# Leading the U steps by 26 columns, the residual in DRAM, one-hots on GpSimd

## The chip, the core and the metric

One core of a Trainium2 chip runs the whole computation in one launch. The metric is the device time of one execution in microseconds. Before the change: median 2835.26 us of 3 runs (2834.31 to 2835.86).

## The reference

512 tokens of width 1024 go through two transformer blocks: the first with two kinds of attention and a gated feed-forward layer, the second with latent and forgetting attention and, in the place of its feed-forward layer, a mixture of single-vector experts. Only this last part is touched. All is float32.

```
qp = h @ w_pq                                  # 8 heads, 2 halves of 128
sc = einsum(qp, sub_keys)                      # 128 scores per head and half
s1, i1 = top_k(sc[0], 16); s2, i2 = top_k(sc[1], 16)
cand = s1[:, None] + s2[None, :]               # 256 sums, top 16 of them
expert = e1 * 128 + e2;  gate = softmax(top_s) # 8 x 16 = 128 slots per token
a = h . peer_u[expert];  w = gate * gelu(a)
y = sum over slots of w * peer_v[expert];  x = x + gate2 * y
```

## The kernel before

The tokens are four tiles of 128. Tiles 0 to 2 take the experts densely, tile 3 takes them sparsely, row by row.

**Dense part.** The 16384 experts are 128 columns of 128 (the column is the second key e2). For column j a *U step* loads `u_by_key[:, j, :]` (512 KB, ring `uraw` of UR = 3 slots), transposes it in two halves on TensorE (`u_transposes`), ScalarE rounds a half to `uT_hi` (`u_high`), VectorE makes the remainder `uT_lo` from PSUM (`u_low`), and TensorE multiplies by the tokens in three passes (`hidden`, 24 matmuls of 384 columns for both halves). `gelu` on ScalarE puts the result into `act_ring`, AHEAD slots of 384 columns. A *V half* (`experts_out`) takes column i's gates times its slot of the ring (`w_mul`), splits product and V column (`w_high`, `w_low`, `v_high`, `v_low`), and adds 18 matmuls of 512 columns into six PSUM banks. The main loop runs over i = 0 to 127 and does V half i and, while i + AHEAD is under 128, U step i + AHEAD. AHEAD is 16: the first 16 U steps run before the loop.

**Gates.** The dense gates are, per token, a 128 by 128 table with 128 entries that aren't zero. First VectorE finds the slots: for 8 heads and 3 tiles `key_tops` and `pair_tops` (one *round*), while TensorE still computes the scores of later heads. `tile_picks` looks the expert numbers up with one-hot tables `hot` of 128 x 2048 and normalises the gates; `slot_transposes` turns them, slot to partition. Then per tile NCH = 16 *chunks* of 8 tokens: VectorE makes `one1` (one instruction of 1024 columns, lines 1526) and eight `one2` (lines 1530, the gate times a one-hot), both in two buffers; TensorE multiplies them (16 matmuls, line 2050), ScalarE moves the result into `stage` (line 896). A tile's `stage` of 8 MB is stored to DRAM by `store_gates` in four transfers, and the next tile's first evacuation waits for them (`stage_free`). The loop reads the gates back, four columns at a time (`load_gates`).

**Where U steps stand before the loop.** One before the lookups, one after them, one after every fourth chunk, the last two after the last chunk.

**Queues.** All loads of U, V and gates and the stores of gates are issued by SyncE in one written order, each behind its own wait: U 0 to 8, store 0, U 9 to 11, store 1, U 12 to 15, store 2, V 0 to 2, gates 0 and 1, U 16 and 17, then the loop's loads. GpSimd has nothing to do between the projections and the loop; in the loop it issues the 256 indirect row loads of tile 3 (three buffers for U rows, three for V rows), whose dot products and sums VectorE makes at fixed steps 4 to 112 (`rows_at`). The last 24 rows in that order are all V rows. `finish3` closes tile 3 at step 112.

**The residual** x (4 x 1024 columns a partition) stays in SBUF throughout.

Of the kernel before, what the change touches and what calls it, by code (L numbers as in the profile page):

```python
# [15 lines left out]
P = 128  # L16
# [22 lines left out]
AHEAD = 16  # L39
# [34 lines left out]
def build(nc, wst, wada, x_in, meta_in, cols_in, rowsa_in, rowsb_in, rope_in, const_in, pos_in,  # L74
          subk_in, peer_u, peer_v, out):
    ctx = ExitStack()
    with ctx:
# [148 lines left out]
        keys = cut(r1, 10752, NKEYS)  # L226
# [7 lines left out]
        act_ring = cut(r2, 0, AHEAD, DN)  # L234
# [14 lines left out]
        hot = cut(big, 0, SLOTS, TOPK)  # L249
        ranks = cut(big, 2048, 2, SLOTS)  # L250
        rank_bits = cut(big, 2304, 2, SLOTS).bitcast(U32)
        topf = cut(big, 2560, 2, PH, TOPK)
        wrap = cut(big, 2816, SLOTS)
        picks = cut(big, 2944, DT, 2, SLOTS)
# [22 lines left out]
        u_by_key, v_by_key = (w.rearrange("(a b) d -> a b d", b=NKEYS) for w in (peer_u, peer_v))  # L277
        gd = nc.dram_tensor("gd", (DT, P, NKEYS * P), F32).ap()
# [55 lines left out]
        y_ready, y_out = sem("y_ready"), sem("y_out")  # L334
# [69 lines left out]

        block = ctx.enter_context(nc.Block())
# [3 lines left out]
        def _(sp):  # L409
# [46 lines left out]
            for j in range(12, 16):  # L456
# [7 lines left out]
            for j in range(AHEAD, AHEAD + 2):  # L464
                load_u(j)
            for i in range(NE):
                if i + AHEAD + 2 < NE:
                    load_u(i + AHEAD + 2)
# [5 lines left out]
            sp.dma_start(out[DT], x[:, DT, :]).then_inc(y_out, 16)  # L474
            for t in range(DT):
                sp.wait_ge(y_ready, t + 2)
                sp.dma_start(out[t], x[:, t, :]).then_inc(y_out, 16)
# [48 lines left out]


# [13 lines left out]
        def _(act):  # L541
# [313 lines left out]
            def gelu(j):  # L855
                act.wait_ge(a_acc, 2 * j + 2)
                if j >= AHEAD:
                    act.wait_ge(w_done, j - AHEAD + 1)
                act.activation(act_ring[:, j % AHEAD, :], ps[:, 0, 0:DN], ACT.Gelu_apprx_tanh,  # L859
                               bias=zero[:]).then_inc(a_ready, 1)  # L860
# [17 lines left out]
            for s in range(3):  # L878
                u_high(s)
            for t in range(DT):  # L880
                act.wait_ge(top_done, 8 * DT - DT + t + 1)
                act.activation(gate[:, t, :], gate[:, t, :], ACT.Exp, bias=zero[:]).then_inc(gate_exp, 1)
            gelu(0)
            for t in range(DT):
                slots_evac(t)
            u_high(3)
            u_high(4)
            gelu(1)
            for t in range(DT):
                stage_free(act, t)  # L890
                for c in range(NCH):
# [6 lines left out]
                    if c % 4 == 3:  # L898
                        j = 2 + 4 * t + c // 4
                        u_high(2 * j + 1)  # L900
                        u_high(2 * j + 2)
                        gelu(j)
            for j in range(2 + 4 * DT, AHEAD):
                u_high(2 * j + 1)
                u_high(2 * j + 2)
                if j < AHEAD - 1:
                    gelu(j)
# [32 lines left out]
        def _(v):  # L940
# [518 lines left out]

            def tile_picks(t):  # L1460

                v.tensor_copy(topf.rearrange("p a h k -> p (a h k)"), topi[:, t, :])
                pair_ranks(besti[:, t, :], rank_bits, ranks, wrap)
                for a in range(2):
                    v.tensor_tensor(hot, over(ranks[:, a, :], TOPK), each(iota, SLOTS), ALU.is_equal)
                    v.drain()
                    hk = hot.rearrange("p (h k) r -> p h k r", h=PH)
                    v.tensor_tensor(hk, hk, topf[:, a].unsqueeze(2).broadcast_to([P, PH, TOPK, TOPK]), ALU.mult)
                    v.drain()
                    v.tensor_reduce(picks[:, t, a, :], hot, AX.X, ALU.add)  # L1470
                    v.drain()
# [6 lines left out]
                v.tensor_tensor(g, g, over(gst[:, 1, PH * t:PH * t + PH], TOPK), ALU.mult)  # L1478
                v.drain().then_inc(picks_ready, 1)
# [11 lines left out]
            def w_mul(i):  # L1491
# [4 lines left out]
                if i >= 2:  # L1496
                    v.wait_ge(v_acc, i - 1)
                v.tensor_tensor(w_of[:, i % 2, :].rearrange("p (t n) -> p t n", t=DT), gring[:, b % 2, :, P * (i % GB):P * (i % GB) + P],
                                act_ring[:, i % AHEAD, :].rearrange("p (t n) -> p t n", t=DT), ALU.mult).then_inc(w_done, 1)
# [5 lines left out]

            for h in range(PH):
# [7 lines left out]
            for s in range(3):  # L1514
                u_low(s)
            for t in range(DT):
                tile_picks(t)
            u_low(3)
            u_low(4)
            for t in range(DT):  # L1520
                v.wait_ge(slot_ready, t + 1)
                for c in range(NCH):
# [5 lines left out]
                    for k in range(CHUNK):  # L1528
                        at = CHUNK * c + k
                        mk = v.tensor_scalar(one2[:, n % 2, k, :], keys, slotT[t][:, P + at:P + at + 1],  # L1530
                                             slotT[t][:, 2 * P + at:2 * P + at + 1], ALU.is_equal, ALU.mult)
                    mk.then_inc(one2_ready, 1)
                    if n and n % 4 == 0:
                        j = 1 + n // 4
                        u_low(2 * j + 1)
                        u_low(2 * j + 2)
            for j in range(1 + 4 * DT, AHEAD):
                u_low(2 * j + 1)
                u_low(2 * j + 2)
# [56 lines left out]
            def finish3():  # L1596
# [6 lines left out]
                v.tensor_tensor(x[:, DT, :], x[:, DT, :], yacc[:, 0, :], ALU.add).then_inc(y_ready, 1)  # L1603
# [5 lines left out]
            for i in range(NE):  # L1609
# [24 lines left out]
                if i == LAST_ROW:  # L1634
                    finish3()

            v.wait_ge(v_acc, NE)
            for t in range(DT):
# [3 lines left out]
                xt = x[:, t, :].rearrange("p (a b) -> p a b", a=2)  # L1642
# [4 lines left out]
        def _(pe):  # L1647
# [374 lines left out]
            def slot_transposes(t):  # L2022
# [4 lines left out]
                for k, src in enumerate((picks[:, t, 0, :], picks[:, t, 1, :], gate[:, t, :])):  # L2027
# [8 lines left out]
            experts_in(0)  # L2036
            for t in range(DT):
                slot_transposes(t)
            experts_in(1)
            for t in range(DT):  # L2040
                for c in range(NCH):
# [11 lines left out]
                    if c % 4 == 3:  # L2053
                        experts_in(2 + 4 * t + c // 4)
            for j in range(2 + 4 * DT, AHEAD):
                experts_in(j)
# [92 lines left out]
```

## Time and profile before

| what | us |
|---|---|
| median of 3 runs | 2835.26 |
| the profiled execution | 2836.87 |
| its span | 2834.8 |
| VectorE's first top-16 round | 1253.2 |
| first gate chunk on TensorE | 1452.3 |
| last gate chunk's end | 1670.5 |
| first instruction of the main loop | 1703.6 |

Busy shares of the span: TensorE 89%, VectorE 63%, ScalarE 34%, GpSimd 13%. The span is the time between the first and the last instruction that the profile shows. The shares are means over stages with different limits, so the rows further down are taken by stage.

In the rows, a window is given as start:end in us from the span's start, and then busy us and instructions in the order TensorE, its weight loads (PEld), VectorE (DVE), ScalarE (ACT), GpSimd (POOL). In a timeline, what stands in brackets is the idle time before the instruction and what ended it. SPq and POOLq are the queues in which SyncE and GpSimd issue transfers.

### The profile page before, as it was taken

Reading aid. Unit: us, or ns where it says so; the run is one execution under the profiler, and the core shown is the slowest. Engines: PE = TensorE matmul, PEld = TensorE weight load, DVE = VectorE, ACT = ScalarE, POOL = GpSimd, SP = SyncE. Lnnn points to the kernel's source line nnn. Section 1 sums busy time; section 2 is a strip of 40 time slices with the busy share of each in tenths; the row PEclk is TensorE's granted clock in tenths of the full one; section 3 lists DMA queues with packets and bytes.
Section 4 is the critical chain, followed back from the end, with each engine's and each line's share of the span. In section 5 each row is a group of like instructions: output and inputs, shape, how many; then the busy total and the mean of one; then the engine's idle time right before and its main releaser. Section 6 shows DMA issues by size and latency. Waiting matters only on the chain.

```text
span 2834.8 us, 37618 instructions
## 1 busy us (share of the span) xinstructions
PE 2533.6 (89%) x13697; PEld 2158.0 (76%) x13697; DVE 1786.0 (63%) x3871; ACT 956.0 (34%) x1637; POOL 354.6 (13%) x326
## 2 busy tenths in 40 slices
PE   8999888999989879989256669999999999999998
PEld 6777686777779757844156668898989898899986
DVE  5535646553254365458887657777777777777675
ACT  4334412222224445311134444333333333333332
POOL 1001100110000000100000001232222222222220
PEclk9999989999999989999678999999999999999999
DMA  4100014652222110030003345787777777778764
GB/s 174 73 31 1 1 62 170 227 203 90 89 74 75 60 45 1 1 126 1 8 23 141 149 175 186 266 291 262 269 261 269 268 265 267 268 272 276 247 222 141
DMA packets 107908, 427.20 MB, mean 151 GB/s; under 512 B 11328, under 2 KB 11584, under 8 KB 97104
## 3 DMA queue, kind: packets, MB, share of 16 engines
q1 hardware_dynamic: 62624, 262.17, 26.3%
q0 software_dynamic: 44064, 160.98, 16.2%
q8 instruction: 111, 1.82, 0.3%
q10 hardware_dynamic: 1040, 1.67, 0.2%
q14 instruction: 69, 0.57, 0.1%
HBM read 397.51 MB, written 27.26 MB: 150 GB/s over the span
## 4 chain that ended last, share of the span: by engine, by line
PE 74%; DVE 14%; issue 4%; ACT 3%; DMA 3%; DVEq 2%; ACTq 1%; SPq 1%; POOLq 0%
PE ps L2017 16%; PE ps L2001 16%; PE ps L1803 9%; PE ps L1757 7%; PE ps L1673 5%; PE ps L1825 4%; PE ps L1990 3%; PE ps L2050 3%; PE ps L1738 2%; DMA gd<-big 1%; PE ps L1942 1%; PE ps L1710 1%; PE ps L1924 1%; ACT r L638 1%; PE ps L1962 1%
## 5 line engine op out<-in xcount | busy, mean ns | idle before, releaser
L2001 PE MATMUL ps<-hd_hi,uT_hi 128*128 128x384 f32 x1024 | 349.9, 342 | 0.7 <-ACT r L859 0.7
L2001 PE MATMUL ps<-hd_hi,uT_lo 128*128 128x384 f32 x1024 | 348.1, 340 | 0.0
L2001 PE MATMUL ps<-hd_lo,uT_hi 128*128 128x384 f32 x1024 | 348.0, 340 | 0.0
L1483 DVE TENSOR_TENSOR uT_lo<-ps,uT_hi 128x512 fp32r<-128x512 f32 x256 | 176.7, 690 | 256.0 <-ACT uT_hi L840 255.8
L2017 PE MATMUL ps<-v_hi,ew_hi 128*128 128x512 f32 x768 | 320.5, 417 | 2.6 <-DVE v_lo L1488 2.1
L2017 PE MATMUL ps<-v_hi,ew_lo 128*128 128x512 f32 x768 | 303.1, 395 | 0.0
L2017 PE MATMUL ps<-v_lo,ew_hi 128*128 128x512 f32 x768 | 300.9, 392 | 0.0
L840 ACT ACTIVATE uT_hi<-ps 128x512 fp32r<-128x512 f32 x256 | 153.1, 598 | 268.8 <-PE ps L1990 268.8
L536 POOL DMA_INDIRECT big<-peer_u,r x128 | 135.3, 1057 | 861.8 <-DVE r L1558 523.5
L859 ACT ACTIVATE r<-ps,zero 128x384 f32<-128x384 f32 x128 | 74.4, 581 | 472.4 <-PE ps L2001 468.1
L1990 PE MATMUL ps<-const,r 128*128 128x128 f32 x1024 | 155.7, 275 | 52.6 <-DVE uT_lo L1483 33.5
L2001 PEld LDWEIGHTS ps<-hd_hi,uT_hi 128*128 128x128 f32 x1024 | 194.0, 189 | 10.0 <-issue 1.1
L2001 PEld LDWEIGHTS ps<-hd_hi,uT_lo 128*128 128x128 f32 x1024 | 193.7, 189 | 9.6
L2001 PEld LDWEIGHTS ps<-hd_lo,uT_hi 128*128 128x128 f32 x1024 | 193.7, 189 | 0.0
L536 POOL DMA_INDIRECT big<-peer_v,r x128 | 144.3, 1127 | 386.2 <-DVE big L1586 369.9
L1488 DVE TENSOR_TENSOR v_lo<-r,v_hi 128x1024 fp32r<-128x1024 f32 x128 | 156.8, 1225 | 34.1 <-ACT v_hi L847 34.1
L1990 PEld LDWEIGHTS ps<-const,r 128*128 128x128 f32 x1024 | 126.7, 141 | 65.7 <-DVE uT_lo L1483 25.5
L1586 DVE SCALAR_TENSOR_TENSOR big<-big,r 128x1024 f32<-128x1024 f32 x128 | 164.5, 1285 | 15.4 <-DMA big<-peer_v,r 3.1
L2017 PEld LDWEIGHTS ps<-v_hi,ew_lo 128*128 128x128 f32 x768 | 144.2, 188 | 32.7
L2017 PEld LDWEIGHTS ps<-v_hi,ew_hi 128*128 128x128 f32 x768 | 144.7, 188 | 26.8 <-DVE v_lo L1488 3.4
L2017 PEld LDWEIGHTS ps<-v_lo,ew_hi 128*128 128x128 f32 x768 | 145.2, 189 | 24.3
L1068 DVE TENSOR_TENSOR w_lo<-big,w_hi 128x2048 fp32r<-128x2048 f32 x42 | 96.2, 2290 | 106.2 <-ACT w_hi L631 106.2
(330 smaller groups left out, 5325.2 us busy)
## 6 DMA issues: line engine op xcount, KB each, us to landing
big<-wst SPq DMA_DIRECT2D x70, 1024.0 KB, 4.9
r<-peer_u SPq DMA_DIRECT2D x128, 512.0 KB, 7.4
r<-peer_v SPq DMA_DIRECT2D x128, 512.0 KB, 5.3
r<-wada POOLq DMA_DIRECT2D x48, 512.0 KB, 4.6
gd<-big SPq DMA_DIRECT2D x12, 2048.0 KB, 14.1
big<-gd SPq DMA_DIRECT2D x32, 768.0 KB, 9.2
x<-x_in SPq DMA_DIRECT2D x4, 512.0 KB, 6.8
big<-peer_u,r POOLq DMA_INDIRECT x128, 6.6
```

The source lines that it names most:

```text
L536: pool.indirect_dma_start(rows[n % RW], None, table, bass.IndirectOffsetOnAxis(ap=idx[:, n:n + 1], axis=0)).then_inc(got[n % RW], 16)
L840: act.activation(uT_hi[:, s % 2], ps[:, 1, :].rearrange("p (k n) -> p k n", k=KD // 2), ACT.Copy).then_inc(u_hi_done, 1)
L1483: v.tensor_tensor(uT_lo[:, s % 2], ps[:, 1, :].rearrange("p (k n) -> p k n", k=KD // 2), uT_hi[:, s % 2].bitcast(F32), ALU.subtract).then_ ...
L1488: v.tensor_tensor(v_lo[:, i % VR, :], vraw[:, i % VR, :], v_hi[:, i % 2, :].bitcast(F32), ALU.subtract).then_inc(v_lo_done, 1)
L1586: v.scalar_tensor_tensor(out=yacc[:, n % 2, :], in0=vrows[n % RW], scalar=wts[:, n:n + 1], in1=yacc[:, n % 2, :], op0=ALU.mult, op1=ALU.ad ...
L1673: mm = pe.matmul(ps[0:r, bank, 0:w], hT[:, k, t * P:t * P + r], wt[:, k, 0:w], start=(k == 0), stop=(k == KD - 1))
L1757: mm = pe.matmul(ps[:, bank, 0:256], h[:, k, t * P:(t + 1) * P], w[:, k, :], start=(k == 0 and i == 0), stop=(k == KD - 1 and i == 2))
L1803: mm = pe.matmul(ps[:, 2 * (f % 2) + u, :], w[:, k, u, :], h[:, k, 0:512], start=(k == 0 and i == 0), stop=(k == KD - 1 and i == 2))
L1825: mm = pe.matmul(ps[:, 2 * t + half, :], a[:, f % 2, t * P:(t + 1) * P], w[:, f % 2, 512 * half:512 * half + 512], start=(f == 0 and i == ...
L1990: mm = pe.transpose(ps[:, 1, P * k:P * k + P], uraw[:, j % UR, at:at + P], ident)
L2001: mm = pe.matmul(ps[:, 0, 0:DN], w[:, k, :], h[:, KD // 2 * half + k, :], start=(half == 0 and k == 0 and i == 0), stop=(half == 1 and k = ...
L2017: mm = pe.matmul(ps[:, 2 + 2 * t + half, :], w[:, P * t:P * t + P], vv[:, 512 * half:512 * half + 512], start=(i == 0 and n == 0), stop=(i ...
```

## The change

- AHEAD is 26. The ring's first ten slots lie in the buffer of the residual x; x is stored to DRAM (`xd`) when the attention's output has been added, and read back (`xback`) at step 116, when tile 3's row buffers are free. ScalarE waits for the store before its first `u_high`.
- U steps before the loop: 11 ahead of the first gate chunk (`u_low` 0 stands before head 6's rounds, then two U steps' `u_low`s behind each of five of the last six rounds, one more behind `tile_ranks(0)`), four in a block behind tile 0's chunks, four behind tile 1's, seven behind tile 2's. None between chunks.
- `tile_picks` is cut in two. `tile_ranks` makes the ranks and, for tile 0, both one-hot tables; `tile_picks` normalises the gates, multiplies and reduces both tables in one instruction. One of tile 0's multiplies runs on GpSimd. The lookups of tiles 1 and 2 stand in VectorE's queue behind `one1` of tile 0's chunks 3 and 8.
- The eight `one2` of every chunk are made by GpSimd; `one1` stays on VectorE.
- SyncE's order: U 0 to 2, the stores of x, U 3 to 13, gates 0, U 14 to 17, gates 1, U 18 to 21, gates 2, V 0 to 2, U 22 to 26, gate loads 0 and 1, U 27 and 28, then the loop's.
- `finish3` is at step 122, after a wait for x.

```diff
-AHEAD = 16
+AHEAD = 26
+INX = 10
+BEFORE = (11, 15, 19, 26)
-        act_ring = cut(r2, 0, AHEAD, DN)
+        x_flat = x.rearrange("p t d -> p (t d)")
+        act_ring = ([x_flat[:, DN * s:DN * s + DN] for s in range(INX)]
+                    + [r2[:, DN * (AHEAD - 1 - s):DN * (AHEAD - s)] for s in range(INX, AHEAD)])
...
# SyncE
-            for j in range(9):
+            for j in range(UR):
+                load_u(j)
+            sp.wait_ge(out_add, 8 * T)
+            for t in range(T):
+                sp.dma_start(xd[t], x[:, t, :]).then_inc(x_out, 16)
+            for j in range(UR, BEFORE[0] + UR):
                 load_u(j)
             store_gates(0)
-            for j in range(9, 12):
+            for j in range(BEFORE[0] + UR, BEFORE[1] + UR):
                 load_u(j)
             store_gates(1)
...
             for i in range(VR):
                 load_v(i)
+            for j in range(BEFORE[2] + UR, AHEAD + 1):
+                load_u(j)
             for b in range(2):
                 load_gates(b)
...
+                if i == LAST_ROW + 4:
+                    sp.wait_ge(u_row, SLOTS)
+                    sp.wait_ge(v_row, SLOTS)
+                    sp.wait_ge(x_out, 16 * T)
+                    for t in range(T):
+                        sp.dma_start(xback[t], xd[t]).then_inc(x_back, 16)
# GpSimd
+            pool.wait_ge(ranks_ready, 1)
+            hk = hot[:, 0].rearrange("p (h k) r -> p h k r", h=PH)
+            pool.tensor_tensor(hk, hk, each_pick(0), ALU.mult).then_inc(hot_ready, 1)
+            for t in range(DT):
+                pool.wait_ge(slot_ready, t + 1)
+                for c in range(NCH):
+                    n = t * NCH + c
+                    if n >= 2:
+                        pool.wait_ge(g_acc, 2 * (n - 1))
+                    for k in range(CHUNK):
+                        at = CHUNK * c + k
+                        mk = pool.tensor_scalar(one2[:, n % 2, k, :], keys, slotT[t][:, P + at:P + at + 1],
+                                                slotT[t][:, 2 * P + at:2 * P + at + 1], ALU.is_equal, ALU.mult)
+                    mk.then_inc(one2_ready, 1)
# ScalarE
+            def hidden_evac(j):
+                u_high(2 * j + 1)
+                u_high(2 * j + 2)
+                gelu(j)
...
+            act.wait_ge(x_out, 16 * T)
+            u_high(0)
+            for j in range(8):
+                hidden_evac(j)
+            gate_exps(0)
+            for j in range(8, 10):
+                hidden_evac(j)
+            gate_exps(1)
+            gate_exps(2)
+            hidden_evac(10)
+            slots_evac(0)
...
# VectorE
+            def tile_ranks(t):
+                v.tensor_copy(topf.rearrange("p a s -> p (a s)"), topi[:, t, :])
+                pair_ranks(besti[:, t, :], rank_bits, ranks, wrap)
+                if t == 0:
+                    for a in range(2):
+                        rank_hot(a).then_inc(ranks_ready, 1)
...
             for h in range(PH):
                 v.wait_ge(sk_ev, 2 * h + 2)
+                if h == PH - 2:
+                    u_low(0)
                 for t in range(DT):
                     key_tops(t, h)
                     v.drain()
                     pair_tops(t, h).then_inc(top_done, 1)
+                    if h >= PH - 2:
+                        u = DT * (h - PH + 2) + t
+                        hidden_low(range(2 * u, min(2 * u + 2, 10)))
+            tile_ranks(0)
+            hidden_low([10])
...
+                    if t == 0 and c in (3, 8):
+                        tile_ranks(c // 5 + 1)
+                        tile_picks(c // 5 + 1)
+                    if t and c == 1:
+                        hidden_low(range(BEFORE[t - 1], BEFORE[t]))
+            hidden_low(range(BEFORE[DT - 1], AHEAD))
# TensorE
+            for j in range(BEFORE[0]):
+                experts_in(j)
+            slot_transposes(0)
...
-                    if c % 4 == 3:
-                        experts_in(2 + 4 * t + c // 4)
+                    if t == 0 and c in (9, 13):
+                        slot_transposes((c - 5) // 4)
+                for j in range(BEFORE[t], BEFORE[t + 1]):
+                    experts_in(j)
```

## Rows read from the trace of the kernel before

**Rows 1.** Windows: length, busy us per engine, granted clock, DMA share, GB/s.

```profile
1253.20:1382.60 129.40, 103.66 (x325) 51.73 (x323) 114.18 (x643) 16.72 (x28) 0.00 (x0) 0.92 0.06 21
1382.60:1450.00 67.40, 16.54 (x73) 15.04 (x73) 53.74 (x63) 8.28 (x14) 0.00 (x0) 0.58 0.05 16
1452.26:1512.13 59.87, 48.59 (x354) 45.99 (x355) 53.92 (x147) 35.15 (x40) 0.00 (x0) 0.97 0.09 27
1512.13:1591.90 79.77, 53.99 (x386) 51.45 (x385) 56.58 (x154) 37.46 (x45) 0.00 (x0) 0.89 0.34 132
1670.54:1703.56 33.02, 13.30 (x81) 12.28 (x79) 3.46 (x5) 4.90 (x9) 0.00 (x0) 0.78 0.95 376
1703.56:2745.00 1041.44, 1032.71 (x5559) 936.37 (x5560) 780.42 (x1311) 365.47 (x590) 279.59 (x256) 1.00 0.75 261
2753.00:2819.40 66.40, 64.28 (x281) 52.31 (x281) 38.63 (x49) 22.59 (x31) 0.00 (x0) 1.00 0.49 155
```

**Rows 2.** The chain that ended last: start us, us, what.

```profile
1450.06 2.05 DVE r L1530 x8
...
1515.62 20.73 DMA gd<-big
...
1594.89 20.20 DMA gd<-big
...
1682.76 20.76 DMA r<-peer_u
```

**Rows 3.** VectorE timeline: start us, us, engine, line, operation, tiles, shapes.

```profile
1392.68 2.29 DVE L1465 TENSOR_TENSOR big<-big,const 128x2048 f32<-128x2048 f32 x1
...
1448.85 1.22 DVE L1526 TENSOR_TENSOR r<-r,gates 128x1024 f32<-128x1024 f32 x1
...
1452.03 1.22 DVE L1526 TENSOR_TENSOR r<-r,gates 128x1024 f32<-128x1024 f32 x1
1453.16 2.13 DVE L1530 TENSOR_SCALAR r<-r,gates 128x128 f32<-128x128 f32 x8
```

**Rows 4.** ScalarE timeline: first uT_hi, then two gelus back to back.

```profile
1359.45 0.60 ACT L840 ACTIVATE uT_hi<-ps 128x512 fp32r<-128x512 f32 x1 [1.03 <-PE ps L1990]
...
1675.75 0.58 ACT L859 ACTIVATE r<-ps,zero 128x384 f32<-128x384 f32 x1 [1.51 <-PE ps L2001]
...
1681.42 0.58 ACT L859 ACTIVATE r<-ps,zero 128x384 f32<-128x384 f32 x1 [1.51 <-PE ps L2001]
```

**Rows 5.** TensorE's timeline: a gate chunk, and the loop's first transposes.

```profile
1461.77 2.02 PE L2050 MATMUL ps<-r 128*128 128x128 f32 x16 [1.16 <-issue]
...
1703.56 1.12 PE L1990 MATMUL ps<-const,r 128*128 128x128 f32 x4 [19.07 <-DMA r<-peer_u]
```

**Rows 6.** GpSimd timeline; last a group of lines (busy us, mean ns).

```profile
329.57 1.89 POOL L489 CAST w_hi<-big 128x2048 fp32r<-128x2048 f32 x1 [57.43 <-ACTq L641]
331.55 4.52 POOL L491 TENSOR_TENSOR w_lo<-big,w_hi 128x2048 fp32r<-128x2048 f32 x1
336.01 2.37 POOL L489 CAST w_hi<-big 128x2048 fp32r<-128x2048 f32 x1
...
L515 POOL MEMSET r<- 128x8 f32 x1 | 0.1, 116 | 4.1 <-issue 4.1
```

**Rows 7.** VectorE's timeline, line 1096: alone, and beside GpSimd's subtract.

```profile
300.37 0.77 DVE L1096 SCALAR_TENSOR_TENSOR r<-r,coef 128x528 f32<-128x528 f32 x1
...
334.02 2.61 DVE L1096 SCALAR_TENSOR_TENSOR r<-r,coef 128x528 f32<-128x528 f32 x1
```

**Rows 8.** Page groups (busy us, mean ns); last, DMA issues of 2700:2750.

```profile
L536 POOL DMA_INDIRECT big<-peer_v,r x128 | 144.3, 1127 | 386.2 <-DVE big L1586 369.9
L1488 DVE TENSOR_TENSOR v_lo<-r,v_hi 128x1024 fp32r<-128x1024 f32 x128 | 156.8, 1225 | 34.1 <-ACT v_hi L847 34.1
...
L1586 DVE SCALAR_TENSOR_TENSOR big<-big,r 128x1024 f32<-128x1024 f32 x128 | 164.5, 1285 | 15.4 <-DMA big<-peer_v,r 3.1
...
big<-peer_v,r POOLq DMA_INDIRECT x12, 5.6
```

More of the change, by code:

```diff
@@ L248, in build @@
         slotT = [gates[:, 0, 0:384], gates[:, 0, 384:768], r1[:, 10240:10624]]
[L249 to L254, printed above, removed]
+        xback = [cut(big, 8192 + D * i, D) for i in range(T)]
+        hot = cut(r2, 0, 2, SLOTS, TOPK)
+        rank_bits = cut(r2, 14368, 2, SLOTS).bitcast(U32)
+        ranks = cut(r2, 14624, 2, SLOTS)
+        wrap = cut(big, NKEYS * P, SLOTS)
+        topf = cut(r1, 11104, 2, SLOTS)
+        picks = [v.rearrange("p (a s) -> p a s", a=2) for v in (gates[:, 0, 768:1024], r1[:, 10848:11104], rowsb[:, 0:256])]
         gring = cut(big, 0, 2, DT, GB * P)
@@ L1458, in pair_ranks, with rank_hot @@
                 v.drain()
-            def tile_picks(t):
[L1462 to L1471, printed above, removed]
+            def rank_hot(a):
+                v.tensor_tensor(hot[:, a], over(ranks[:, a, :], TOPK), each(iota, SLOTS), ALU.is_equal)
+                return v.drain()
+            def tile_ranks(t):
[4 more added lines that the diff above has]
+                        rank_hot(a).then_inc(ranks_ready, 1)
+            def tile_picks(t):
                 v.wait_ge(gate_exp, t + 1)
@@ L1478, in tile_picks @@
                 v.tensor_tensor(g, g, over(gst[:, 1, PH * t:PH * t + PH], TOPK), ALU.mult)
+                for a in ((0, 1) if t else (1,)):
+                    if t:
+                        rank_hot(a)
+                    hk = hot[:, a].rearrange("p (h k) r -> p h k r", h=PH)
+                    v.tensor_tensor(hk, hk, each_pick(a), ALU.mult)
+                    v.drain()
+                if t == 0:
+                    v.wait_ge(hot_ready, 1)
+                v.tensor_reduce(picks[t], hot, AX.X, ALU.add)
                 v.drain().then_inc(picks_ready, 1)
@@ L1504, in w_low, with hidden_low @@
                                 ALU.subtract).then_inc(ew_lo_done, 1)
+            def hidden_low(steps):
+                for j in steps:
+                    u_low(2 * j + 1)
+                    u_low(2 * j + 2)
             for h in range(PH):
                 v.wait_ge(sk_ev, 2 * h + 2)
+                if h == PH - 2:
+                    u_low(0)
                 for t in range(DT):
@@ L1511, in _ @@
                     pair_tops(t, h).then_inc(top_done, 1)
+                    if h >= PH - 2:
[3 more added lines that the diff above has]
+            hidden_low([10])
             v.wait_ge(keys_acc, 1)
             v.tensor_scalar(keys, ps[:, 2, 0:NKEYS], 1.0, None, ALU.subtract)
[L1514 to L1519, printed above, removed]
+            v.drain()
+            tile_picks(0)
             for t in range(DT):
@@ L2026, in slot_transposes @@
                     pe.wait_ge(slot_ready, t - 1)
-                for k, src in enumerate((picks[:, t, 0, :], picks[:, t, 1, :], gate[:, t, :])):
+                for k, src in enumerate((picks[t][:, 0, :], picks[t][:, 1, :], gate[:, t, :])):
                     mm = pe.transpose(ps[:, 2 + t % 2, P * k:P * k + P], src, ident)
@@ L2052, in _ @@
                         mm.then_inc(g_acc, 1)
[L2053 to L2056 removed]
+                    if t == 0 and c in (9, 13):
+                        slot_transposes((c - 5) // 4)
+                for j in range(BEFORE[t], BEFORE[t + 1]):
+                    experts_in(j)
             for i in range(NE):
```

68 lines of the change are left out of this document (23 added, 45 removed).

## The prediction

> **What bounds the kernel now.** I read the busy time by stage first. In the loop over key columns TensorE is the bound: 112 steps in about 1041 us, 9.3 us each, and after them 16 steps without a U half in 66.4 us, 4.15 us each [rows 1]. Before that loop it is not: 1253 to 1450 us is VectorE's stretch, and in the gate stage TensorE is busy for 48.6 of 59.9 us of tile 0 and 54.0 of 79.8 of tile 1. The chain of waits names what ends last there [rows 2]: VectorE's one-hot builds, two 20 us waits while 8 MB of gates are stored, and a 20.8 us transfer of a U column queued behind the third store, for which TensorE idles 19.1 us [rows 5]. VectorE gives its prices [rows 1, 3]: one top-16 round 5.39 us (24 rounds in 129.4), one pass over a 2048-wide one-hot 2.29 us, and per chunk of 8 experts one1 1.22 us and eight one2 2.13 us, pitch 3.18 us. TensorE's 16 matmuls of a chunk are 2.02 us [rows 5], so the chunk is VectorE's. One U step back to back takes 5.67 us, gelu to gelu [rows 4].
>
> I sum against the profiled execution (2836.87 us, span 2834.8), which is 1.6 us above the median 2835.26.
>
> **Term 1, up to the first gate chunk.** VectorE starts u_low(0) ahead of head 6, about 18 rounds after 1253.2, at 1350.2. But ScalarE makes the first uT_hi at 1359.45 [rows 4], behind all score evacuations, and that order is kept. VectorE waits and is done at 1360.8, 10.6 us lost. Then six rounds (32.3 us) with five groups of four u_lows. The first of a group finds its input ready (0.69 us); the three others wait for transposes, the 2.1 us of matmuls, gelu and ScalarE: about 7.5 us. Five groups are 41 us. Between groups TensorE pauses some 2.5 us; a transpose batch after a pause took 1.12 us, and the clock was 0.58 over the pauses of 1382 to 1450 [rows 1, 5]; I add 7 us. That is 1441. tile_ranks(0) with two hots 6.8; the eleventh step's two u_lows 3; gate sums, one multiply (2.29) and one 4096-wide reduction (two passes, 4.5) 8.5; slot transposes and evacuation 1.5: 1460. GpSimd's one multiply there costs 4.5 us [rows 6], hidden by those u_lows but for a fraction. GpSimd then needs a first chunk of one2, and TensorE starts it at 1463 instead of 1452.3: +10.7 us, with 11 U steps done instead of 2.
>
> **Term 2, the pitch of a chunk.** The trace has no tensor_scalar on GpSimd. Its ends: a one-input pass costs 1.89 us for 2048 elements and a tiny one 0.116, so 128 elements are 0.23 us; by the two-input pass (4.52) 0.39 [rows 6]. It has one tensor input but two operations and two per-partition scalars, so I take 0.30, between the ends. Now the shared access: VectorE's two-input L1096 takes 0.77 us alone and 2.61 when it starts during GpSimd's subtract; it ends 0.56 after that one, and GpSimd's next cast takes 2.37 instead of 1.89 [rows 6, 7]. So the two take turns. one1 has two SBUF inputs and runs once per chunk, 1.15 us taken from GpSimd. Pitch: 8 x 0.30 + 1.15 = 3.55 us, ends 2.96 and 4.27, against 3.18 now. Moving one2 gains nothing, since the free VectorE can't hurry GpSimd.
>
> The Trainium skill says the same of the pair ("SBUF — State Buffer", Who interferes with whom): an exclusive lock, held for a whole instruction, also against a VectorE instruction with two SBUF inputs. By its figure for one-input work ("GPSIMD Engine Reference", Engine selection: roughly line rate) the pitch would be at my lower end.
>
> **Term 3, the gate stage.** Tile 0: 15 pitches + 2.0 = 55.3. The lookups of tiles 1 and 2 stand in VectorE's queue ahead of the next one1: 17 us each (four passes 9.4, reduction 4.5, the rest 3) and 1 for turns. GpSimd can only be two chunks ahead, since one2 has two buffers. Chunk 4 starts 19.2 us after chunk 3's one1, chunk 6's one2 begins 2.2 later: a delay of 21.4 - 2 x 3.55 = 14.3 us, twice 28.6. Tile 0 ends at 1463 + 83.9 = 1546.9.
>
> Between tiles four U steps run in a block. The ring has three U columns; the fourth is issued behind the 8 MB store. Two steps take 12 us, the third stops at 14.9 in the transposes of column 14. The store is issued 1.2 after the last chunk and lands some 23 us later (20.7 in flight, rows 2), the column at 25.7: 10.8 us idle. Then 2.6 + 5.7 + 2 (low clock) = 36 us to the next tile's first chunk. The tile: 36 + two prepared chunks 4.1 + 14 x 3.55 = 89.8 us; now tile 1 takes 79.8 [rows 1] and tile 2 the same (its store's wait starts 79.3 us after the first's, rows 2), also with four U steps each, because there the steps lie mostly inside VectorE's pitch. Ends: 1636.7 and 1726.5.
>
> After tile 2, seven U steps. Two run, the third waits for a column that is issued behind the store and three V columns, which lands at about 28 us; then 2.6 + 2 + 4 x 5.67 = 27.3. The loop begins at 1726.5 + 55.3 = 1781.8 instead of 1703.56: **+78.2 us**.
>
> **Term 4, the loop.** Ten U steps fewer: steps 102 to 111 have only the V half, 4.15 us of TensorE instead of 9.26. But tile 3's rows go on to step 112, 256 rows over 108 steps = 2.37 a step, and the last 24 are all V rows through three buffers: issue 1.13, landing 5.6 from issue, VectorE 1.29 [rows 8], with hand-overs about 8 us for three, 6.4 us a step. (VectorE's own sum is below: 2.37 x 1.29, v_low 1.23 and two 384-wide passes near 0.5 each, 5.3.) So the saving is 10 x (9.26 - 6.4) = **-28.6**, ends -20 and -38. The residual's 2 MB read at step 116 puts a V load about 5 us later, which had about as much slack: +1. Its store at 1260 us is beside projections: 0. finish3's three passes move into equal steps: 0.
>
> Sum: 78.2 - 28.6 + 1 = +51; 2836.87 + 51 - 1.6 = **2886 us** (on the median's footing).
>
> Each 0.1 us of one2 is 0.8 us a chunk; in the terms above about 40 pitches count, 32 us. Ends: 0.23 gives 2862, 0.39 gives 2915. The ends of term 1 (0 to +16 for clock and pauses) and of term 4 add about 15 to each side.
>
> **Rivals.**
> A, faster: GpSimd keeps ahead and TensorE is the chunk's bound, at 2.1 us. It decides where eight one2 and their turns are below 2.3 us, so 0.23 each and no turns with one1. 40 x (3.55 - 2.1) = 58 less: 2828. For it: TensorE needs only 2.02; against it: rows 7. Chance 0.14.
> B, GpSimd is much dearer: the per-partition scalars are fetched anew for each instruction, one2 at 0.5 us, pitch 5.15, 40 x 1.6 = 64 more: 2950. For it: no row shows such an instruction, and the small ones have a fixed share of 0.1; against: nothing here shows a fixed share that large. Chance 0.16. The Trainium skill ("GPSIMD Engine Reference", Performance pitfalls for Q7 kernels) charges each small read about 102 cycles; by that two scalars would add 0.17 us to 0.23, near 0.40, between the forecast and B.
> C, the column isn't held by the store (it overtakes): 2 x 10.8 + 11 less, 2854. Against: TensorE's 19.1 us wait [rows 5]. Chance 0.08.
> D, the change doesn't put lookups beside gates in a useful way: this is already in the sum (28.6 us). If they hid wholly: 2858, chance inside the forecast's low side.
>
> The forecast with its ends: chance 0.62, 2862 to 2915. Faster by over 0.2% (what this kernel's measurement can tell, 5.7 us) holds most of A and little of C: 0.15; within 0.2%: 0.04; slower 0.81. Range 2828 to 2945: below lies half of A, above most of B's half.
>
> **What would show it.** Right: eight one2 on GpSimd fill the chunk, with one1 lengthened; u_low(0) waits about 10 us; a stop of TensorE near 11 us on a peer_u transfer within each block between tiles; two 14 us holes in tile 0; steps 102 to 111 above 6 us. First gate chunk near 1463, loop near 1782. Wrong: a chunk pitch under 3 us, or a loop start before 1725 (then it is faster), or steps 102 to 111 at 4.2 us (22 us better).

## The result, and the profile after

The change makes the kernel slower: 3046.2 us median of 4 runs (3045.8 to 3051.3) against 2835.6 (2834.3 to 2836.1, one run more than ahead of the prediction), ratio 1.075; the brackets give the 95% interval, [1.074, 1.077]. The forecast was 2886 us, with a range from 2828 to 2945. The sign was right and most places were right; one price was wrong by a factor of 2.6, and it was paid for 48 chunks.

The windows of the changed kernel by stage (length, then busy us of TensorE, weight loads, VectorE, ScalarE, GpSimd, granted clock, DMA share, GB/s), to lay beside [rows 1]:

```profile
1253.20:1382.60 129.40, 122.66 (x412) 67.97 (x411) 96.61 (x530) 23.13 (x38) 0.00 (x0) 0.97 0.13 45
1382.60:1474.87 92.27, 52.64 (x287) 48.07 (x285) 54.54 (x159) 21.45 (x34) 12.96 (x10) 0.81 0.16 52
1474.87:1599.20 124.33, 59.66 (x263) 55.84 (x264) 51.89 (x45) 33.24 (x33) 124.33 (x125) 0.60 0.00 0
1599.20:1634.40 35.20, 23.07 (x130) 21.91 (x129) 6.76 (x9) 7.11 (x12) 9.66 (x12) 0.84 0.74 298
1634.40:1741.70 107.30, 54.57 (x259) 51.37 (x258) 18.48 (x15) 32.60 (x32) 105.27 (x118) 0.64 0.00 0
1741.70:1777.20 35.50, 24.08 (x130) 22.93 (x130) 6.76 (x9) 7.11 (x12) 9.60 (x12) 0.83 0.74 296
1777.20:1883.00 105.80, 54.05 (x258) 50.75 (x257) 17.36 (x14) 32.56 (x32) 100.53 (x112) 0.66 0.00 0
```

The three long windows are the tiles' chunks. In tile 0 GpSimd is busy for 124.33 of 124.33 us, TensorE for 59.66, VectorE for 51.89. Where VectorE bounded the chunks before, GpSimd does now, without a gap. The group on the page and GpSimd's timeline over tile 0 (start, duration, what) say it again (the first row of the timeline is the one multiply, 4.48 us for 4.5 forecast). The page's mean of 971 ns holds the turns with VectorE as well, in which the two engines wait for each other:

```profile
L563 POOL TENSOR_SCALAR r<-r,gates 128x128 f32<-128x128 f32 x256 | 243.9, 971 | 42.7 <-PE ps L2110 27.6
```

```profile
1446.83 4.48 POOL L554 TENSOR_TENSOR r<-r 128x2048 f32<-128x2048 f32 x1 [225.92 <-DVEq L1509]
1466.39 94.00 POOL L563 TENSOR_SCALAR r<-r,gates 128x128 f32<-128x128 f32 x89 [15.08 <-ACT gates L915]
```

TensorE's timeline of the changed kernel, to lay beside [rows 5]. Lines 2110 are a chunk's 16 matmuls, 2051 the transposes of a U step:

```profile
1474.87 3.75 PE L2110 MATMUL ps<-r 128*128 128x128 f32 x16 [9.11 <-POOL r L563]
1482.11 3.75 PE L2110 MATMUL ps<-r 128*128 128x128 f32 x16 [3.49 <-POOL r L563]
1489.39 3.75 PE L2110 MATMUL ps<-r 128*128 128x128 f32 x16 [3.52 <-issue]
1502.81 3.75 PE L2110 MATMUL ps<-r 128*128 128x128 f32 x16 [9.67 <-issue]
...
1545.04 3.75 PE L2110 MATMUL ps<-r 128*128 128x128 f32 x16 [9.45 <-issue]
...
1624.85 0.69 PE L2051 MATMUL ps<-const,r 128*128 128x128 f32 x2 [11.15 <-DMA r<-peer_u]
...
1912.86 0.69 PE L2051 MATMUL ps<-const,r 128*128 128x128 f32 x2 [15.56 <-DMA r<-peer_u]
```

From 1474.87 to 1482.11 is 7.24 us: the pitch of a chunk, 3.18 before. The two longer gaps (9.67 and 9.45) are the lookups of tiles 1 and 2, then come the stops on a U column behind a store. Only the first two gaps name GpSimd; the others are put down to "issue". The chain of waits alone would mislead here, since it follows TensorE, VectorE's one1 and then "issue":

```profile
1482.11 3.77 PE ps L2110 x16
1485.90 1.27 DVE r L1592
1487.17 2.21 issue
1489.39 3.75 PE ps L2110 x16
1493.14 9.67 issue
```

one1 waits for the buffer that the chunk before frees, and the "issue" behind it is the time in which GpSimd finishes its eight. The windows' GpSimd column is what settles it.

The gap of 9.67 us is made by the two engines' turns. While VectorE makes and multiplies the one-hot tables of a lookup (four passes with two inputs), GpSimd gets one instruction done per pass (GpSimd's row, then VectorE's of the same time):

```profile
1489.27 11.11 POOL L563 TENSOR_SCALAR r<-r,gates 128x128 f32<-128x128 f32 x5
```

```profile
1490.14 2.28 DVE L1508 TENSOR_TENSOR r<-r,const 128x2048 f32<-128x2048 f32 x1
...
1497.33 2.38 DVE L1532 TENSOR_TENSOR r<-r 128x2048 f32<-128x2048 f32 x1
```

Five one2 take 11.11 us, where five alone take 3.9. The same happens to VectorE ahead of the gates: its two one-hot tables of tile 0 take 9.05 us, where one alone is 2.29 [rows 3], because GpSimd's multiply (4.48 us from 1446.83) starts ahead of the second.

```profile
1444.41 9.05 DVE L1508 TENSOR_TENSOR r<-r,const 128x2048 f32<-128x2048 f32 x2
```

The first `uT_lo` of VectorE with its wait, and the waits from 2894.16 to 2966.76, ten steps without a U half (engine, line, what it waited for: us in total, times, longest):

```profile
1364.57 0.69 DVE L1541 TENSOR_TENSOR uT_lo<-ps,uT_hi 128x512 fp32r<-128x512 f32 x1 [8.97 <-ACT uT_hi L879]
```

```profile
POOL big L575 <- DVE big L1646: 43.4, 15, 7.3
PEld ps L2078 <- DVE v_lo L1546: 22.9, 9, 6.2
PE ps L2078 <- DVE v_lo L1546: 18.8, 7, 5.8
...
DVE big L1646 <- DMA big<-peer_v,r: 6.9, 4, 2.9
```

There TensorE waits for VectorE, whose queue holds the row work between the V halves. Ten such steps take 72.6 us; the same ten, still with their U halves, took 90.9 before:

```profile
2662.40:2753.33 90.93, 90.93 (x491) 82.51 (x490) 64.52 (x76) 29.73 (x49) 24.37 (x22) 1.00 0.71 248
```

### The profile page after: what moved, and what is told of

Its sections match the earlier page's. It is cut to its first block, busy times and chain, and to the rows that moved or that the text cites. A ratio compares the mean times of both kernels' runs of the same rounds, so it can differ in the third digit from the quotient of the medians.

```text
span 3049.5 us, 37605 instructions
## 1 busy us (share of the span) xinstructions
PE 2629.1 (86%) x13697; PEld 2237.1 (73%) x13697; DVE 1696.9 (56%) x3483; ACT 967.5 (32%) x1640; POOL 722.6 (24%) x711
## 4 chain that ended last, share of the span: by engine, by line
PE 73%; DVE 11%; issue 6%; ACT 3%; DMA 3%; DVEq 1%; POOL 1%; ACTq 1%; SPq 0%
PE ps L2062 14%; PE ps L2078 14%; PE ps L1864 8%; PE ps L1818 6%; PE ps L2110 5%; PE ps L1734 5%; PE ps L1886 4%; PE ps L2023 4%; PE ps L2051 3%; DMA r<-peer_u 2%; DVE r L1592 2%; PE ps L1799 2%; PE ps L1771 1%; PE ps L2003 1%; PE ps L1985 1%
## 5 line engine op out<-in xcount | busy, mean ns | idle before, releaser
L2110 PE MATMUL ps<-r 128*128 128x128 f32 x768 | 167.6, 408 | 178.3 <-issue 165.7
L2110 PEld LDWEIGHTS ps<-r 128*128 128x128 f32 x768 | 156.8, 312 | 189.0 <-issue 189.0
L563 POOL TENSOR_SCALAR r<-r,gates 128x128 f32<-128x128 f32 x256 | 243.9, 971 | 42.7 <-PE ps L2110 27.6
L944 ACT ACTIVATE big<-ps 128x512 f32<-128x512 f32 x96 | 99.8, 1053 | 247.6 <-PE ps L2110 247.6
```

The lines of the kernel that those rows point to most:

```text
L563: mk = pool.tensor_scalar(one2[:, n % 2, k, :], keys, slotT[t][:, P + at:P + at + 1], slotT[t][:, 2 * P + at:2 * P + at + 1], ALU.is_equal ...
L2110: mm = pe.matmul(ps[:, 4 + u % 4, P * k:P * k + P], one1[:, n % 2, 4 * half + k, :], one2[:, n % 2, 4 * half + k, :], start=True, stop=True)
```

## The experiments

**One2 back on VectorE, the rest of the change kept.** The eight `tensor_scalar` move from GpSimd's list to behind `one1`:

```diff
-                        mk = pool.tensor_scalar(one2[:, n % 2, k, :], keys, ...
+                        mk = v.tensor_scalar(one2[:, n % 2, k, :], keys, ...
```

> The changed kernel with only the eight one2 of a chunk back on VectorE. Theory S (a GpSimd one2 at 0.905 us was the mis-sized term, the rest of the sum stands): chunk pitch near 3.2 us instead of 7.24, two lookups in tile 0 that cost about 14 us each, two blocks of 35 us between tiles, loop steps 102 to 111 at 7.3 us; 2875 to 2895 us, still slower than before. Rival R (the one2 hid a good change: the ten U steps moved out of the loop pay): below 2830 us.

Measured: 2888.7 us (2885.3 to 2889.7), ratio 1.018 [1.016, 1.020]; theory S holds and rival R falls. So GpSimd's share of the loss is 157.5 us of 210.6, and the rest of the change costs 53. TensorE's timeline of this kernel (its gate line is 2104):

```profile
1470.12 2.02 PE L2104 MATMUL ps<-r 128*128 128x128 f32 x16 [1.60 <-issue]
1473.30 2.02 PE L2104 MATMUL ps<-r 128*128 128x128 f32 x16 [1.16 <-issue]
1493.49 5.44 PE L2104 MATMUL ps<-r 128*128 128x128 f32 x32 [18.17 <-issue]
...
1526.76 3.76 PE L2104 MATMUL ps<-r 128*128 128x128 f32 x16 [17.82 <-issue]
...
1574.35 0.47 PE L2045 MATMUL ps<-const,r 128*128 128x128 f32 x1 [8.01 <-DMA r<-peer_u]
```

The pitch is 3.18 again. Here the lookups are dear, gaps of 18.2 and 17.8 us for 1.2 to 1.6 elsewhere, so about 17 us each, the forecast's own price of a lookup: with one2 behind them in the same queue nothing is prepared meanwhile. "Lookups beside the gate matmuls" hides almost nothing of them. The last row is the stop behind tile 0's store, there without GpSimd too.

**The kernel before, with one2 on GpSimd alone.** The same move in the other direction:

```diff
+                        mk = pool.tensor_scalar(one2[:, n % 2, k, :], keys, ...
-                        mk = v.tensor_scalar(one2[:, n % 2, k, :], keys, ...
```

> The kernel before with only the eight one2 of a chunk on GpSimd, nothing else of the change. Theory S: chunk pitch near 7.2 us, three tiles near 120 to 130 us each with U steps hidden under GpSimd's time, so the gate stage 150 to 160 us longer: 2980 to 3000 us. Rival R (the pitch comes from the change's order of lookups and U steps around the chunks): under 2900 us.

Measured: 2960.9 us (2958.7 to 2964.7), ratio 1.044 [1.042, 1.045], far above rival R's 2900 and 19 us below the expectation's low end. The pitch of this kernel, on TensorE's timeline:

```profile
1488.35 3.75 PE L2057 MATMUL ps<-r 128*128 128x128 f32 x16 [4.34 <-issue]
1495.58 3.75 PE L2057 MATMUL ps<-r 128*128 128x128 f32 x16 [3.48 <-issue]
```

It is 7.23 us, as in the changed kernel, so the price comes with the eight one2 on GpSimd (and one1 beside them) and from nothing else in the change. Nearly the whole cost follows: 48 chunks at 7.24 are 348 us, where the three tiles took 59.9 + 79.8 + about 79.3 = 219 with their U steps [rows 1, 2]. That is +129; +125.3 was measured. The U steps between the chunks cost nothing now, because TensorE does them while GpSimd works. The expectation had that, but took 120 to 130 us for a tile where 16 pitches are 116.

**What makes the instruction dear: three kernels with other forms.** Each takes the changed kernel, gives GpSimd another form in each tile, and leaves `one1` out from chunk 2 on (8 columns are written in its place), so that outside the lookups hardly anything takes turns with GpSimd. What they compute is no longer the gates; only their traces are read.

```diff
-                    v.tensor_tensor(one1[:, n % 2], each(keys, CHUNK), ...
+                    if n < 2: (as before)
+                    else: v.tensor_scalar(one1[:, n % 2, 0, 0:8], keys[:, 0:8], 0.0, None, ALU.add)
# first kernel: tile 0 as in the change; tile 1 constants; tile 2 twice as wide, 4 a chunk
+                            mk = pool.tensor_scalar(one2[:, n % 2, k, :], keys, 5.0, 0.5, ALU.is_equal, ALU.mult)
+                            mk = pool.tensor_scalar(one2[:, n % 2, 2 * k:2 * k + 2, :], each(keys, 2), ...
# second kernel: tile 0 one comparison; tile 1 with a constant; tile 2 two inputs
+                            mk = pool.tensor_scalar(..., keys, slotT[t][:, P + at:P + at + 1], None, ALU.is_equal)
+                            mk = pool.tensor_scalar(..., keys, 5.0, None, ALU.is_equal)
+                            mk = pool.tensor_tensor(..., keys, slotT[t][:, ...].broadcast_to([P, NKEYS]), ALU.mult)
# third kernel: tile 0 a multiply; tile 1 twice as wide; tile 2 a wide comparison
+                            mk = pool.tensor_scalar(one2[:, n % 2, k, :], keys, 0.5, None, ALU.mult)
```

> The changed kernel, one1 left out from chunk 2 on (an 8-column one-input write stands for it). Tile 0: one2 as it is. Tile 1: both scalars are constants in the instruction. Tile 2: per-partition scalars, four instructions of 256 columns for eight of 128. Theory F (fetching two per-partition scalars is a fixed cost): tile 0 at 0.90 us each, tile 1 at 0.25 to 0.45, tile 2 at 1.0 to 1.1. Rival E (two operations on each element are slow): tile 1 stays at 0.9, tile 2 near 1.7. Rival T (turns with VectorE's one1): tile 0 falls to 0.76 and the pitch from 7.24 to 6.1 us.

> As the run before, one1 left out. Tile 0: one comparison with one per-partition scalar. Tile 1: one comparison with a constant. Tile 2: a two-input multiply of 128 columns. Theory F: tile 0 midway between 0.9 and the constants' time (0.55 to 0.7 us), tile 1 0.25 to 0.4, tile 2 near 0.39. Rival E: tile 0 and tile 1 alike, near 0.5.

> GpSimd's forms again, one1 left out, gates meaningless. Tile 0: one multiply by a constant, 128 columns; tile 1: the same, 256 columns; tile 2: one comparison with a constant, 256 columns. Two-input multiplies of 128 columns took 0.36 us, comparisons 0.59. Theory C (the comparison is the slow part): tile 0 near 0.25 us, tile 1 near 0.36, tile 2 near 0.95. Theory G (every tensor_scalar takes this slow path, whatever its operation): tile 0 near 0.59, tile 1 and 2 alike, 0.9 to 1.0.

Measured: 2973.4, 2917.5 and 2890.1 us, one run each. What counts is GpSimd's timeline, one stretch of back-to-back instructions after another; a stretch divided by its count is one instruction. First kernel:

```profile
1615.90 78.90 POOL L567 TENSOR_SCALAR r<-r 128x128 f32<-128x128 f32 x112 [30.39 <-PE ps L2119]
...
1736.07 67.23 POOL L569 TENSOR_SCALAR r<-r 128x256 f32<-128x256 f32 x56 [31.55 <-PE ps L2119]
```

Second kernel:

```profile
1591.45 66.24 POOL L566 TENSOR_SCALAR r<-r 128x128 f32<-128x128 f32 x112 [30.60 <-PE ps L2118]
...
1697.87 14.33 POOL L568 TENSOR_TENSOR r<-r 128x128 f32<-128x128 f32 x40 [34.34 <-PE ps L2118]
```

Third kernel:

```profile
1518.20 26.23 POOL L563 TENSOR_SCALAR r<-r 128x128 f32<-128x128 f32 x53
...
1584.41 45.63 POOL L565 TENSOR_SCALAR r<-r 128x256 f32<-128x256 f32 x56 [33.45 <-PE ps L2116]
...
1669.90 51.07 POOL L567 TENSOR_SCALAR r<-r 128x256 f32<-128x256 f32 x56 [32.53 <-PE ps L2116]
```

A stretch of tile 0 counts only outside the two lookups, whose passes stretch GpSimd's instructions; the third kernel's row starts behind the second lookup. For the first two kernels I take TensorE's pitch of a chunk over 8: 6.18 us in the first, 4.63 in the second (3.95 in the third, the same 0.49 as its row). In us per instruction:

| GpSimd instruction | 128 columns | 256 columns |
|---|---|---|
| two operations, two per-partition scalars (the change) | 0.773 | 1.20 |
| two operations, two constants | 0.705 | |
| one comparison, per-partition scalar | 0.578 | |
| one comparison, constant | 0.592 | 0.912 |
| one multiply, constant | 0.494 | 0.815 |
| multiply of two inputs, the second one column repeated | 0.358 | |

Four things follow. Leaving one1 out shortens the chunk by 7.24 - 6.18 = 1.06 us, so the two do take turns, at the forecast's 1.15 but for a tenth (rival T of the first expectation). The scalars in memory aren't the price: 0.773 against 0.705 with both constant, and 0.578 against 0.592, so theory F falls. A doubled width adds 0.32 to 0.43, so 128 columns carry a part that no width explains, if cost grows in a straight line between the two widths: 0.773 - (1.20 - 0.773) = 0.35 us of the change's instruction, 0.27 of the comparison, 0.17 of the lone multiply. And the operation counts: a comparison costs 0.10 more than a multiply at either width, and the second operation some 0.11, so the third expectation's theory G (every form alike, near 0.59) is wrong as well as its theory C (0.25). Every one-input form is dearer than the two-input one, the reverse of [rows 6]. Why that is so stays open, and no run made one2 of wide two-input passes.

The second kernel's tile 0 shows a lookup again: its second one delays the next chunk to 12.07 us after the last, at a pitch of 4.63.

```profile
1506.99 2.02 PE L2118 MATMUL ps<-r 128*128 128x128 f32 x16 [1.27 <-DVE r L1601]
1519.06 1.20 PE L2118 MATMUL ps<-r 128*128 128x128 f32 x4 [10.05 <-issue]
```

**Tile 3's rows earlier.** The kernel with one2 on VectorE, and one more edit:

```diff
-FIRST_ROW, LAST_ROW = 4, 112
+FIRST_ROW, LAST_ROW = 4, 101
```

> The run with one2 on VectorE, and the last of tile 3's 256 rows at step 101 instead of 112 (2.6 rows a step; finish3 and the read of x move along by 11 steps). Theory S (steps 102 to 111 are held by V rows through three buffers, 7.3 us each where TensorE needs 4.15): those steps fall to 4.2 us and the whole by 25 to 32 us, to about 2860 us. Rival L (the rows cost the same wherever they stand, because the loop's VectorE or DMA has no room): no gain, 2880 to 2890 us.

Measured: 2875.4 us (2871.2 to 2878.0), ratio 1.014 [1.012, 1.017]; 13.3 less than without it, half of what theory S expected. Windows of the first (112) and the second (101): steps 2 to 50, then ten steps without a U half.

```profile
1786.83:2233.98 447.15, 443.28 (x2392) 401.55 (x2391) 340.93 (x622) 161.56 (x259) 120.96 (x112) 1.00 0.77 264
2728.71:2804.40 75.69, 52.44 (x196) 40.23 (x195) 52.53 (x57) 15.18 (x21) 26.96 (x22) 0.86 0.72 245
```

```profile
1789.01:2250.28 461.27, 448.75 (x2401) 405.12 (x2400) 363.76 (x683) 165.06 (x262) 137.95 (x124) 0.99 0.78 270
2745.44:2793.49 48.05, 47.03 (x207) 38.20 (x206) 26.93 (x34) 15.33 (x21) 0.00 (x0) 1.00 0.58 198
```

The ten late steps fall from 75.7 to 48.1 us, all that was hoped for (27.6). But the 48 early ones rise by 14.1: 12 more row DMAs and 23 us more of VectorE stand in them (some of tile 3's top-16 searches come along with the rows), and TensorE, busy for 443.3 of 447.2 before, now has 12.5 us without work, all of it waiting for `uT_lo`. The rate of 2.6 rows a step alone doesn't explain it: the next 50 steps take up 11 more row DMAs and rise by only 2.8 us (466.6 to 469.4).

**U columns between the parts of a store.** On the kernel with one2 on VectorE (behind tile 2, gate load 0 also moves ahead of V 1 and 2):

```diff
-            store_gates(0)
-            for j in range(BEFORE[0] + UR, BEFORE[1] + UR):
-                load_u(j)
+                store_quarter(t, 0)
+                store_quarter(t, 1)
+                load_u(a + UR)
+                store_quarter(t, 2)
+                load_u(a + UR + 1)
+                store_quarter(t, 3)
...
```

> The run with one2 on VectorE, and the U columns a block needs issued between the four quarters of a tile's gate store instead of behind it; after tile 2 the first gate columns ahead of V 1 and 2. Theory S (a block stops 8 to 12 us, the last one 15 us, for a column behind the store): the stops on peer_u go, blocks take 25 us instead of 36, and the time falls by 25 to 35 us, to about 2858 us. Rival W (the stores only move the stop: the next tile's first evacuation then waits as long): under 8 us of gain.

Measured: 2862.1 us (2858.9 to 2869.2), ratio 1.009 [1.006, 1.011]: 26.6 less by the medians, 19.6 by the profiled spans (2867.4 and 2887.0). TensorE's waits for a U column between the gate stage and the loop, without the edit and with it:

```profile
PE ps L2045 <- DMA r<-peer_u: 32.2, 3, 15.4
```

```profile
PE ps L2052 <- DMA r<-peer_u: 10.9, 3, 8.4
```

21.3 us of stops are gone, and the loop begins 19.0 earlier, nearly all of the 19.6 of the spans; the rest of the 26.6 lies within the spread of the runs. Rival W falls. Between the tiles the columns were held by the order of SyncE's queue: the stops of 8.0 and 8.8 us are gone. Behind tile 2 some 10 us are left of 15.4.

**All of it put in another order.** Lead 26 is kept. one2 and all lookups are VectorE's and the lookups stand ahead of the first chunk, with `u_low`s put singly between their pieces; 14 U steps are ahead of the gate stage; `u_low(0)` is behind round 20 of 24 and not ahead of round 19, so that it needn't wait so long; the stores are split; rows end at 101.

```diff
-BEFORE = (11, 15, 19, 26)
-FIRST_ROW, LAST_ROW = 4, 112
+BEFORE = (14, 18, 22, 26)
+FIRST_ROW, LAST_ROW = 4, 101
-                    if t == 0 and c in (3, 8):
-                        tile_ranks(c // 5 + 1)
-                        tile_picks(c // 5 + 1)
+            for t in range(DT):
+                tile_ranks(t)
+                next_low()
+                tile_picks(t)
...
```

> The lead of 26 kept, everything around it reordered: one2 and all lookups on VectorE ahead of the gates, single u_lows between the pieces of the rounds and lookups so that VectorE does not wait (14 U steps ahead of the gates), u_low 0 only behind round 20, blocks of four U steps with split stores, rows done at step 101. Theory S by its own terms: first gate chunk near 1475 us, chunk pitch 3.2, blocks of 25, loop start near 1710, 102 x 9.3 + 26 x 4.15 behind it: 2775 to 2795 us, faster than before by 40 to 60. Rival: each u_low between pieces waits for TensorE's 2.8 us pace and the first gate chunk comes 15 us later, 2800 us.

Measured: 2787.8 us (2785.8 to 2790.3), ratio 0.983 [0.981, 0.985]. It is 1.7% faster than the kernel before and beats the changed one by 8.5%. Its windows: up to the first chunk, tile 0, and the block behind it.

```profile
1382.60:1458.78 76.18, 63.50 (x357) 55.84 (x357) 68.50 (x103) 24.10 (x41) 0.00 (x0) 0.98 0.24 76
1458.78:1508.80 50.02, 33.27 (x255) 31.02 (x256) 49.49 (x139) 29.48 (x31) 0.00 (x0) 0.97 0.00 1
1508.80:1533.70 24.90, 21.48 (x132) 20.36 (x131) 10.06 (x23) 7.55 (x13) 0.00 (x0) 1.00 0.92 369
```

The first chunk starts 16 us before the changed kernel's, with three U steps more behind it; tile 0 takes 50.0 instead of 124.3, the block 24.9 instead of 35.2. The loop's first multiply is at 1688.26; before it was at 1705.95. The expectation's 2775 to 2795 was met partly by luck: the loop starts some 20 us earlier than its 1710, and the loop's steps are slower than its 9.3 us (steps 2 to 50 take 9.57).

**The same with rows to step 112,** to see whether the early rows pay there too:

```diff
-FIRST_ROW, LAST_ROW = 4, 101
+FIRST_ROW, LAST_ROW = 4, 112
```

> The reordered kernel (lead 26, one-hots and lookups on VectorE ahead of the gates, 14 U steps ahead of the first gate chunk, U columns between the parts of a store) with tile 3's rows spread to step 112 again instead of 101. By the two runs that differ in this alone under the other order (2888.7 with 112, 2875.4 with 101), theory E (early rows pay in the tail what they cost in part in the loop, independent of the order ahead of the loop): steps 2 to 50 at 9.31 us instead of 9.57, steps 101 to 111 at 7.3 to 8.3 instead of 5.35, together 2796 to 2806, so 10 to 15 slower than 2787.8. Theory F (the slower loop steps of the reordered kernel come from something else than the rows, so that they stay near 9.57): 2808 to 2820.

Measured: 2802.8 us (2800.1 to 2803.5), ratio 0.988 [0.986, 0.990]; 15.0 more. Steps 2 to 50 and ten late steps:

```profile
1700.05:2147.56 447.51, 443.55 (x2394) 401.83 (x2393) 341.22 (x622) 161.60 (x259) 121.92 (x112) 1.00 0.78 264
2642.14:2715.82 73.68, 53.72 (x198) 40.67 (x197) 52.56 (x58) 15.18 (x21) 30.22 (x22) 0.88 0.75 255
```

The ten late steps take 73.7 us instead of 48.0, steps 2 to 50 take 447.5 instead of 459.5. So the exchange is the same in both orders: 26 to 28 us won late for 12 to 14 given early. The slower early steps come from the rows and what moves with them (theory E).

## Why the prediction was wrong, point by point

The stages from the first chunk to the loop, in us:

| | forecast | measured |
|---|---|---|
| start of the first gate chunk | 1463 | 1474.9 |
| tile 0's chunks | 83.9 | 124.3 |
| block of four U steps | 36 | 35.2 |
| tile 1's chunks | 53.8 | 107.3 |
| block of four U steps | 36 | 35.5 |
| tile 2's chunks | 53.8 | 105.8 |
| from there to the loop | 55.3 | 54.2 |
| the loop starts later by | 78.2 | 233.7 |

**The step that failed: Term 2, "so I take 0.30, between the ends".** One `tensor_scalar` of 128 columns costs GpSimd 0.773 us alone and 0.905 with the turns; the pitch is 7.24, not 3.55, and not within the ends either (4.27). The forecast's own rule, 40 pitches, gives 40 x 3.69 = 148 us more, 2886 + 148 = 3034 of 3046. The mistake wasn't in which number was taken but in the ends: both came from another kind of instruction (a cast, a two-input subtract) at a large size, scaled down by columns. An instruction with two operations and a scalar operand had no row, and the text said so; then the honest upper end isn't the next dearer elementwise pass but a multiple of it. With some 40 pitches of eight, 0.1 us was worth 32 us, and that alone should have made the range wider on the slow side. The lower end of the range, at 2828, rested on a case (GpSimd faster than VectorE) that no `tensor_scalar` measured here comes near (0.494 at best).

**Rival B** (0.5 us, 2950) was nearest, for a wrong reason: its fetch of scalars is 0.07 us where both go, and nothing where one does. **Rival A** fell: TensorE needs its 2 us but GpSimd 6.2 even without turns. **Rival C** fell: the column is held, 11.15 us forecast as 10.8. **Rival D** fell too: with one2 on VectorE a lookup costs its full 17 us.

**The turns** between one1 and one2 were right: 1.06 us a chunk for 1.15. In the lookups they were put at 1 us or less, and one lookup's four passes hold GpSimd for some 7 us (Terms 1 and 3). The rule quoted from the Trainium skill ("SBUF — State Buffer", Who interferes with whom) agrees with these traces: beside a two-input pass of 2.3 us GpSimd's instructions lie 2.47 us apart, for 0.773 alone. Its other rule ("GPSIMD Engine Reference", Engine selection: one input at roughly line rate) doesn't hold for these forms: 0.49 us for one multiply of 128 columns, and the two-input one is cheaper. The measurement decides.

**Term 1** was right up to the end of the rounds (1442.6, forecast 1441; `u_low(0)` waited 9.0 us and was done at 1365.3, forecast 1360.8, because TensorE came to it some 4 us later). Then `tile_ranks(0)` took 10.9 us (1442.6 to 1453.5) instead of 6.8: GpSimd's multiply, put as hidden but for a fraction, held the second one-hot table. So the slots were ready at 1466.4 instead of 1460, and the first chunk came 8.5 us behind them instead of 3, for the first eight one2.

**Term 3** was right in the blocks: they are within 1 us, and the stop behind tile 2's store is 15.6 us. The lookups came out near its formula by luck. With a pitch of 7.24 it gives 21.4 - 2 x 7.24 = 6.9 us, and the gaps are 9.6 for 3.5, so 6.1. But its mechanism, a late one1, isn't what delays the chunk: GpSimd works on that chunk's one2 all the while and is slowed by the four two-input passes. The three kernels with other forms tell the two apart. There a lookup delays TensorE by 6.8 to 8.2 us at pitches of 6.18, 4.63 and 3.95, where the formula gives 9.0, 12.1 and 13.5 (about 1 less without one1). So the 28.6 us for two lookups at a pitch of 3.55 was probably too much; no run has that pitch.

**Term 4** had the right cause and a size too good: ten steps take 72.6 instead of 90.9, so -18 and not -28.6, at 7.3 us a step for 6.4. The estimate saw three V rows in flight but not that VectorE's row work makes TensorE wait for `v_lo` (18.8 us in ten steps). Even the steps without rows take 4.8 us each (48.05 for ten), not 4.15.

**The rest of the sum** stands in its sign, not to the microsecond. The kernel with one2 on VectorE is the change without Term 2's price. Its loop starts 68.2 us later than before and its late steps save 90.9 - 75.7 = 15.2, together +53.0; +52.8 was measured, so these two places hold the whole loss. The forecast's own terms with a pitch of 3.18 give 78.2 - 15 = 63 for the start and -28.6 for the late steps, 2871 us, 18 too few: 13 of them are Term 4's, 5 the start's. So the change is slower even with one2 at VectorE's price.

**Where the gain of a longer lead went.** A lead of 26 moves ten U halves, 10 x 5.1 us, out of the loop; they need idle TensorE time ahead of it. The blocks give them none: with one2 on VectorE, TensorE waited 32 us there for columns (37 in the changed kernel) and the steps stood alone, not beside VectorE's chunks. In the tail the ten V halves that were left ran into rows instead (27.6 us). The lookups, meant to run beside the matmuls, held the next chunk (about 34 us). Each was undone or avoided in the reordered kernel, and 2888.7 became 2787.8. How the 101 us divide over the edits made together was shown for two only (20 to 27 for the stores, 13 to 15 for the rows); the others (lookups ahead, `u_low`s singly, 14 steps ahead) were not run apart.

## What to carry to other kernels

Before work goes to an engine, find a row of that very form on that engine; without one, take an upper end that is a multiple, not a neighbour, and multiply it by the count before anything else is worked out. Spare time on an engine is worth nothing to an instruction that costs it three times as much and that stands in every turn of a loop. Where two engines take turns, look for the longest passes of the one beside the other, not only for the pair that meets in every turn of the loop. In this kernel a larger lead paid once the early steps lay beside another engine's work and their loads weren't queued behind a store.

## What the runs showed of the hardware

- GpSimd's `tensor_scalar` on 128 x 128 fp32 took 0.49 to 0.77 us, of it 0.17 to 0.35 independent of the width (by a straight line through 128 and 256 columns); VectorE did the change's eight in 2.13 us, 0.27 each [rows 3]. A multiply of two inputs, the second one column repeated, took GpSimd 0.358.
- VectorE's one1 (1.22 us) beside GpSimd's eight one2 lengthened the chunk by 1.06 us, nearly the whole of one1. Beside VectorE's two-input passes of 2048 columns (2.3 us each) GpSimd got one `tensor_scalar` done per pass, 2.47 us apart instead of 0.773.
- The clock that was granted to TensorE in tile 0 was 0.60 on the mean, where it was 0.97 before, and 0.50 over the second chunk (1482.20 to 1489.30). With 3.5 us of idle time between chunks 16 matmuls took 3.75 us instead of 2.02, the lower of the two levels (1.2 and 2.4 GHz), and with 1.16 us between them 2.02. It cost next to nothing here, since GpSimd set the pitch, but a busy share of TensorE (59.7 of 124.3 us) read without the clock would have overstated its load almost twofold.
